# Last three experts of a mixture layer summed by tokens on TensorE, in a one-core hybrid encoder layer

## What is computed

```python
    g_w, g_idx = lax.top_k(group_prob, 1)
    e_w, e_idx = lax.top_k(e_prob, MOE_TOPK)
    weights = g_w * e_w / jnp.sum(e_w)
    hid = silu(h @ w1[e]) * (h @ w3[e])        # 1024 -> 256
    out = sum over the two chosen e of weight * (hid @ w2[e])
    x = x + gt2 * out                          # gt2: a row of 1024, from c
    return rms_norm(x, final_norm_g)
```

## Time and profile before

| | |
|---|---|
| time, median of 3 runs | 794.81 us (790.16 to 795.22) |
| time of the profiled execution | 794.91 us |
| its span, first to last instruction | 792.9 us |
| granted TensorE clock, mean over the span | 0.958 of full |
| TensorE busy | 715.3 us, 90% |
| VectorE busy | 371.7 us, 47% |
| ScalarE busy | 283.9 us, 36% |
| data moved by DMA | 206.94 MB, mean 261 GB/s |

### The profile page before, as it was taken

One profiled execution on the slowest core, in us unless ns is written; L12 is line 12 of the kernel. 1 busy time (PEld: TensorE's weight loads), 2 busy tenths in 40 slices (PEclk: granted clock), 3 DMA queues, 4 the chain that ended last, 5 costly groups with the idle time before them and its releaser, 6 DMA issues.

```text
span 792.9 us, 12682 instructions
## 1 busy us (share of the span) xinstructions
PE 715.3 (90%) x5356; PEld 566.0 (71%) x5356; DVE 371.7 (47%) x648; ACT 283.9 (36%) x406; POOL 43.5 (5%) x39
## 2 busy tenths in 40 slices
PE   9999999999999969889999999989999988888740
PEld 7889999987777757668999998865555554545320
DVE  3476877844564596666677457434201010100006
ACT  2256544565454341243635334332222222222101
POOL 0010000000000714400000000000000000000010
PEclk9999999999999988899999999999999999999985
DMA  9954765755656431222554457968999999999933
GB/s 372 412 199 135 264 238 181 266 212 213 249 218 223 150 117 57 88 74 104 167 207 157 162 195 292 421 273 357 417 422 424 423 421 423 421 424 421 421 88 134
DMA packets 33691, 206.94 MB, mean 261 GB/s; under 512 B 4177, under 2 KB 4561, under 8 KB 10466
## 3 DMA queue, kind: packets, MB, share of 16 engines
q1 hardware_dynamic: 27218, 193.00, 62.7%
q10 hardware_dynamic: 5120, 8.39, 3.0%
q0 software_dynamic: 1296, 4.72, 1.6%
HBM read 194.57 MB, written 11.53 MB: 260 GB/s over the span
## 4 chain that ended last, share of the span: by engine, by line
PE 66%; DMA 18%; DVE 9%; ACT 2%; issue 2%; SPq 2%; DVEq 0%; POOL 0%; ACTq 0%; POOLq 0%
PE ps L1344 65%; DMA r_z<-in_expert_pieces 7%; DMA ring<-in_expert_pieces 4%; DMA r_bt<-in_expert_pieces 4%; SPq L412 2%; DVE ring_rounded L847 2%; ACT ring_rounded L554 2%; DMA ring<-in_pieces 1%; PE ps L1464 1%; DVE r_pv L1033 1%; DVE r_pv L1035 1%; DMA r_lm<-y_rows,r_btm 1%; DMA r_xs<-in_x_t 1%; DVE newton L832 0%; PE ps L1736 0%
## 5 line engine op out<-in xcount | busy, mean ns | idle before, releaser
L847 DVE TENSOR_TENSOR ring_rounded<-ring,ring_rounded 128x2048 fp32r<-128x2048 f32 x60 | 139.6, 2332 | 104.1 <-ACT ring_rounded L554 104.0
L1344 PE MATMUL ps<-hT_rounded,ring_rounded 128*128 128x256 f32 x832 | 156.6, 288 | 0.9 <-DVE ring_rounded L847 0.9
L554 ACT CAST ring_rounded<-ring 128x2048 fp32r<-128x2048 f32 x60 | 114.1, 1903 | 66.8 <-DMA ring<-in_pieces 37.2
L1344 PEld LDWEIGHTS ps<-hT_rounded,ring_rounded 128*128 128x128 f32 x832 | 133.1, 195 | 3.6 <-issue 2.2
L1344 PE MATMUL ps<-x_sb_rounded,ring_rounded 128*128 128x256 f32 x416 | 119.0, 286 | 0.0
L1344 PE MATMUL ps<-ring_rounded,hT_rounded 128*128 128x512 f32 x352 | 111.1, 397 | 0.0
L1287 DVE COPY r_pv<-ps 128x128 f32<-128x128 f32 x32 | 9.3, 292 | 196.4 <-PE ps L1736 196.4
L1344 PEld LDWEIGHTS ps<-x_sb_rounded,ring_rounded 128*128 128x128 f32 x416 | 81.2, 195 | 0.2 <-issue 0.2
L1344 PE MATMUL ps<-ring,r_lm 128*64 128x256 f32 x512 | 67.3, 388 | 13.1 <-DMA ring<-in_expert_pieces 11.0
L1344 PEld LDWEIGHTS ps<-ring_rounded,hT_rounded 128*128 128x128 f32 x352 | 66.1, 190 | 15.3 <-issue 1.8
L1344 PEld LDWEIGHTS ps<-ring,r_lm 128*64 128x64 f32 x512 | 44.1, 140 | 38.0 <-issue 24.2
(11 more groups left out here) (296 smaller groups left out, 1046.1 us busy)
## 6 DMA issues: line engine op xcount, KB each, us to landing
ring<-in_pieces SPq DMA_DIRECT2D x76, 1024.0 KB, 5.0
ring<-in_expert_pieces SPq DMA_DIRECT2D x48, 1024.0 KB, 27.2
r_z<-in_expert_pieces SPq DMA_DIRECT2D x12, 1024.0 KB, 22.5
r_xs<-in_expert_pieces SPq DMA_DIRECT2D x12, 1024.0 KB, 24.2
y_rows<-r_st ACTq DMA_DIRECT2D x64, 128.0 KB, 7.1
g_sb<-in_expert_pieces SPq DMA_DIRECT2D x6, 1024.0 KB, 24.0
r_st<-in_expert_pieces SPq DMA_DIRECT2D x6, 1024.0 KB, 25.4
r_bt<-in_expert_pieces SPq DMA_DIRECT2D x6, 1024.0 KB, 27.8
```

Source lines behind the costliest of these rows:

```text
L554: nc.scalar.copy(high_of(p_), slot_of(p_)).then_inc(hi_ok, 1)
L847: nc.vector.tensor_tensor(low_of(p_), slot_of(p_), high_of(p_).bitcast(F32), ALU.subtract).then_inc(lo_ok, 1)
L1344: return nc.tensor.matmul(o, l, r, start=start, stop=stop)
```

## The change

- Experts 0 to 28 (`EARLY_E` = 29) go the old way, with VectorE in place of ScalarE reading the down product from PSUM; it multiplies by gt2 while it does (`output` is now VectorE's, `gt2_two` holds the row in the layout of `y_row`). ScalarE issues the stores (`store`).
- Experts 29, 30 and 31 are not stored. VectorE makes for them, beside expert 28, weighted one-hot matrices of tokens by slots (`late_pick`: 6 instructions of 128x128 and 4 small ones), TensorE transposes them after the up products of expert 29 (6 transposes into banks 4 and 5), VectorE copies them to `late_rows`, and `scatter(e)` multiplies: 4 products, with 64 rows of weights of 128 columns and 512 columns of the output, accumulated over the three experts in banks 4 to 7. Their input rows in `y_rows` are zero filled beforehand (`ZERO_PARTS`: 6 transfers near 51 us, of which the last is a half, for 4).
- The branch for extra windows stands between expert 28 and expert 29 on TensorE, VectorE and ScalarE. SP waits for the stores up to expert 28, so the gathers are released ahead of the last experts. `y_two` moves to `r_z`.
- The order of TensorE from there is: turn 29, down 29, up 30, scatter 29, turn 30, down 30, up 31, scatter 30, turn 31, down 31, scatter 31. Output 30 waits for `moe_done`.
- VectorE adds the gathered rows of t = 0 to x before output 31, those of t = 1 after it, and then four halves of 128x512 from banks 4 to 7; squares, scalings and the sending of the output go by halves of 512 columns, with one more small addition ahead of the Newton steps.

```diff
+LATE = 3
+EARLY_E = E - LATE
+ZERO_PARTS = ((LATE + JOBS) * W + P - 1) // P
...
-        gt2b = view(r_q, "p d -> p d")
+        gt2_two = r_q[:, 0:CW]
...
-        y_two = view(r_lm, "p (t c d) -> p t c d", t=TT, c=2)
+        y_two = view(r_z, "p (t c d) -> p t c d", t=TT, c=2)
+        late_pick = r_lm[:, 512:512 + LATE * TT * P].rearrange("p (e t h r) -> p e t h r", e=LATE, t=TT, h=2)
+        late_rows = r_lm[:, 1280:1280 + LATE * TT * P].rearrange("p (e t n) -> p e t n", e=LATE, t=TT)
...
-                sp.wait_ge(y_stored[k], 32 * (E // 4))
+                sp.wait_ge(y_stored[k], 32 * len(range(k, EARLY_E, 4)))
             sp.wait_ge(jobs_ok, 1)
-            sp.wait_ge(rows_zeroed, 16 * (JOBS * W // P))
+            sp.wait_ge(rows_zeroed, 16 * ZERO_PARTS)
...
-                sp.wait_ge(fin_done, t + 1)
-                sp.dma_start(out[0, t * P:(t + 1) * P, :], x_sb[:, t]).then_inc(out_done, 16)
-            sp.wait_ge(out_done, 16 * TT)
+                for h in range(2):
+                    sp.wait_ge(fin_done, 2 * t + h + 1)
+                    sp.dma_start(out[0, t * P:(t + 1) * P, h * CW:(h + 1) * CW], x_sb[:, t, h * CW:(h + 1) * CW]).then_inc(
+                        out_done, 16)
+            sp.wait_ge(out_done, 16 * 2 * TT)
...
-            for i in range(JOBS * W // P):
-                pool.dma_start(y_rows[E * W + i * P:E * W + (i + 1) * P, :], zeros).then_inc(rows_zeroed, 16)
+            for i in range(ZERO_PARTS):
+                lo = EARLY_E * W + i * P
+                hi = min(lo + P, (E + JOBS) * W)
+                pool.dma_start(y_rows[lo:hi, :], zeros[0:hi - lo]).then_inc(rows_zeroed, 16)
...
-            def output(e):
-                act.wait_ge(down_full, e + 1)
-                if e >= 2:
-                    act.wait_ge(y_stored[(e - 2) % 4], 32 * ((e - 2) // 4 + 1))
-                nc.scalar.copy(y_row[:, e % 2], ps[2 + e % 2][:]).then_inc(y_out, 1)
+            def store(e):
                 act.wait_ge(y_out, e + 1)
                 for h in range(2):
                     act.dma_start(y_rows[e * W:(e + 1) * W, h * CW:(h + 1) * CW], y_row[h * W:(h + 1) * W, e % 2]).then_inc(
...
-            for e in range(E):
-                if e + 1 < E:
-                    silu_of(e + 1)
+            for e in range(EARLY_E):
+                silu_of(e + 1)
                 if e + 5 < E:
                     rows_of_quarter(e + 5)
-                output(e)
+                store(e)
             act.wait_ge(jobs_ok, 1)
...
-                    act.wait_ge(x_down, j)
-                    nc.scalar.copy(y_row[:, 0], ps[2][:]).then_inc(x_out, 1)
-            for t in range(TT):
-                act.wait_ge(y_sum, t + 1)
-                if t:
-                    act.wait_ge(x3_sq, t)
-                nc.scalar.activation(sq_end, x_sb[:, t], ACT.Square, accum_out=st[:, 4 + t:5 + t]).then_inc(x3_sq, 1)
+            for e in range(EARLY_E + 1, E):
+                silu_of(e)
+            for t in range(TT):
+                for h in range(2):
+                    n_sq = 2 * t + h
+                    act.wait_ge(y_sum, n_sq + 1)
+                    if n_sq:
+                        act.wait_ge(x3_sq, n_sq)
+                    at = 10 + 2 * h + t
+                    nc.scalar.activation(sq_end[:, 0:CW], x_sb[:, t, h * CW:(h + 1) * CW], ACT.Square,
+                                         accum_out=st[:, at:at + 1]).then_inc(x3_sq, 1)
...
+                    half = slice(h * W, (h + 1) * W)
+                    if w == 1:
+                        ins = nc.vector.tensor_copy(gt2_two[half], bank[half, :])
+                    else:
+                        ins = nc.vector.tensor_copy(gt1b[:, h * 512:(h + 1) * 512], bank[:])
+                    ins.then_inc(mix_used(("gtb", w, h)), 1)
...
+            def output(e):
+                dve.wait_ge(down_full, e + 1)
+                if 2 <= e < EARLY_E + 2:
+                    dve.wait_ge(y_stored[(e - 2) % 4], 32 * ((e - 2) // 4 + 1))
+                if e == EARLY_E + 1:
+                    dve.wait_ge(moe_done, 1)
+                if e >= EARLY_E + 2:
+                    dve.wait_ge(late_sum, e - EARLY_E - 1)
+                nc.vector.tensor_tensor(y_row[:, e % 2], ps[2 + e % 2][:], gt2_two, ALU.mult).then_inc(y_out, 1)
+
+            def picks_of_late_experts():
+
+                for t in range(TT):
+                    link(nc.vector.tensor_scalar(ix[:, 6, 0:LATE], ohG[:, 2 * t, EARLY_E:], R[17][:, t, 0:1], None, ALU.mult))
+                    link(nc.vector.scalar_tensor_tensor(late_w[:, t], ohG[:, 2 * t + 1, EARLY_E:], R[18][:, t, 0:1],
+                                                        ix[:, 6, 0:LATE], ALU.mult, ALU.add))
+                    for i in range(LATE):
+                        nc.vector.tensor_scalar(late_pick[:, i, t], count1.unsqueeze(1).to_broadcast([P, 2, W]),
+                                                rank1[:, t, EARLY_E + i:EARLY_E + i + 1], late_w[:, t, i:i + 1],
+                                                ALU.is_equal, ALU.mult).then_inc(late_ok, 1)
+
+            def rows_of_late_experts():
+
+                dve.wait_ge(late_turned, 1)
+                flat = late_rows.rearrange("p e t n -> p (e t n)")
+                nc.vector.tensor_copy(flat[:, 0:512], ps[4][:])
+                nc.vector.tensor_copy(flat[:, 512:], ps[5][:, 0:(LATE * TT - 4) * P]).then_inc(late_back, 1)
+
             hidden(0)
-            for e in range(E):
+            for e in range(EARLY_E):
                 if e % 4 == 2 and e // 4 + 2 < E // 4:
                     pick_quad(e // 4 + 2)
                 hidden_turned(e)
-                if e + 1 < E:
-                    hidden(e + 1)
+                hidden(e + 1)
+                if e == EARLY_E - 2:
+                    picks_of_late_experts()
+                output(e)
...
+            rows_of_late_experts()
             dve.wait_ge(jobs_ok, 1)
             extra = dve.value_load(jobs_i[0:1, JOBS:JOBS + 1], min_val=0, max_val=JOBS)
             with dve.If(extra > 0):
...
-
-            for t in range(TT):
+                    dve.wait_ge(x_down, j)
+                    nc.vector.tensor_tensor(y_row[:, 0], ps[2][:], gt2_two, ALU.mult).then_inc(x_out, 1)
+
+            def add_gathered(t):
                 dve.wait_ge(y_two_ok[t], 32)
-                link(nc.vector.scalar_tensor_tensor(y_two[:, t, 0], y_two[:, t, 1], R[12][:, t, 0:1], y_two[:, t, 0],
-                                                    ALU.mult, ALU.add))
-                link(nc.vector.scalar_tensor_tensor(y_two[:, t, 0], y_two[:, t, 0], R[17][:, t, 0:1], gt2b, ALU.mult,
-                                                    ALU.mult))
-                nc.vector.tensor_tensor(x_sb[:, t], x_sb[:, t], y_two[:, t, 0], ALU.add).then_inc(y_sum, 1)
+                for c_ in range(2):
+                    link(nc.vector.scalar_tensor_tensor(x_sb[:, t], y_two[:, t, c_], R[17 + c_][:, t, 0:1], x_sb[:, t],
+                                                        ALU.mult, ALU.add))
+
+            hidden_turned(EARLY_E)
+            output(EARLY_E)
+            hidden(EARLY_E + 1)
+            hidden_turned(EARLY_E + 1)
+            output(EARLY_E + 1)
+            hidden(E - 1)
+            hidden_turned(E - 1)
+            add_gathered(0)
+            output(E - 1)
+            add_gathered(1)
+            for t in range(TT):
+                for h in range(2):
+                    dve.wait_ge(late_sum, LATE + t)
+                    half = x_sb[:, t, h * CW:(h + 1) * CW]
+                    nc.vector.tensor_tensor(half, half, ps[4 + 2 * t + h][:], ALU.add).then_inc(y_sum, 1)
             dve.wait_ge(s_fng, 16)
-            dve.wait_ge(x3_sq, TT)
+            dve.wait_ge(x3_sq, 2 * TT)
+            link(nc.vector.tensor_tensor(st[:, 4:6], st[:, 10:12], st[:, 12:14], ALU.add))
             rstd(st[:, 4:4 + TT], D)
             for t in range(TT):
-                nc.vector.scalar_tensor_tensor(x_sb[:, t], x_sb[:, t], st[:, 4 + t:5 + t], fng, ALU.mult,
-                                               ALU.mult).then_inc(fin_done, 1)
+                for h in range(2):
+                    half = slice(h * CW, (h + 1) * CW)
+                    nc.vector.scalar_tensor_tensor(x_sb[:, t, half], x_sb[:, t, half], st[:, 4 + t:5 + t], fng[:, half], ALU.mult,
+                                                   ALU.mult).then_inc(fin_done, 1)
...
-            for e in range(E):
-                if e + 1 < E:
-                    up_of(e + 1)
+            def scatter(e):
+
+                pe.wait_ge(y_out, e + 1)
+                if e == EARLY_E:
+                    pe.wait_ge(late_back, 1)
+                for t in range(TT):
+                    for h in range(2):
+                        part = slice(h * W, (h + 1) * W)
+                        ins = mm(ps[4 + 2 * t + h][:], late_rows[part, e - EARLY_E, t], y_row[part, e % 2], e == EARLY_E, e == E - 1)
+                    if t == TT - 1 or e == E - 1:
```

(51 more changed lines are left out.)

## The result

The changed kernel takes 781.54 us (median of 4 runs, 779.96 to 783.95) where the kernel before, run beside it on the same chip, takes 793.59 (4 runs, 790.16 to 795.22): ratio 0.9856, 95% interval 0.981 to 0.9902. Forecast were 786.0 and a range of 782.8 to 790.0.

A forecast was written before the change was run, and what follows sets the result against it. The chain of waits was taken as the bound, with wins only behind 754.5: 13.4 us won after the last down product, 2.8 lost, 794.9 - 10.6 = 784.3, plus 1.7 for a fallen clock = 786.0; range 782.8 to 790.0.

The forecast's parts named there:

- the clock: Between turn 29 and down 29: a 2.0 to 3.1 us gap halves TensorE's clock once, costing 1.7 us; chance 0.37.
- Work ahead of expert 28: Before expert 28: VectorE's output reads, larger zero fill and picks are hidden, costing nothing; 1.2 us if cover were gone.
- Turn 28 to down 29: TensorE after the up products of expert 29: transposes, down 28 ending at 745.5, down 29 starting at 748.2.
- half price of VectorE's branch: Ahead of down 29: VectorE's register load and branch could cost 0 to 1.1 us; half was taken, giving 748.2.
- Down 29 to D: TensorE from down 29 to D, the last down product's end: D at 766.4, 2.8 us later than before.
- The gathers: Released after expert 28's stores at 755.4, first half in at 762.7: hidden with 1.7 us to spare.
- D to the end: From the last down product's end to the kernel's end: 15.9 us instead of 29.3, so 13.4 won.
- the term of the last square: Behind the last down product's end (D): last 128x512 square, 0.63 plus hand-over, follows VectorE's additions, done at D+7.5.
- rival 2: Branch ahead of turn 29 stalls if new instructions must be fetched: 786.6 to 791.6 us; chance 0.10.
- rival 5: From 745.5 to the end of the matmuls the clock stays at 1.2 GHz: 802 us, slower; chance 0.04.
- rival 1: The sum without a fallen clock: 784.3 us; chance 0.27.

The follow-up runs named there:

- before again: The kernel before the change, unchanged, measured once more for its own spread: 790.41 us (8 runs), ratio 0.9981.
- after: The changed kernel as first measured and profiled: 781.54 us, ratio 0.9856 to the kernel before the change; its profiled execution took 780.43.
- no-branch kernel: Changed kernel without the count load, branch and extra-window loop on TensorE, VectorE and ScalarE, and without SP's loop: ratio 0.9849 to the kernel before the change.
- after again: The changed kernel, unchanged, measured and profiled once more: 780.69 us (4 runs), ratio 0.9856 to the kernel before the change.
- two late experts: Changed kernel with experts 30 and 31 summed on TensorE instead of three experts, 29 being stored: ratio 0.9848 to the kernel before the change.
- before: The kernel without the change, run beside the changed one: 793.59 us (4 runs); its first profiled execution took 794.91.
- four late experts: Changed kernel with experts 28 to 31 summed on TensorE and the first gathered half added earlier: ratio 0.9858 to the kernel before the change.
- four, shorter release: Changed kernel with experts 28 to 31 summed on TensorE, SP's count read earlier, a semaphore per gather, gathered passes in VectorE's idle times: 782.8 us, ratio 0.9874.

## Why the prediction was right on where the gain lies and too high in its time

The failed step is the clock: a fall to half clock between turn 29 and down 29 was costed at 1.7 us and measured at nothing. Of the 4.5 us between the 786.0 forecast and 781.54, 1.7 are this term, 1.3 the base of the sum, 0.5 the sum itself, and 1.0 stays open.

The base of the sum was the one profiled execution: 794.91, which I took as typical because the shown median was 794.81. Other sets of the same kernel have medians of 793.59, 791.5 and 791.88. The profiled execution held more low-clock time than before again, and my gain was subtracted from it.

Point by point. Times of after are given on the scale of the forecast, with 3.34 added, by which its transposes at 738.81 stand ahead of the 742.15 of the earlier trace rows.

- **Work ahead of expert 28**: costed at nothing. From the first selection product to turn 28 it grew by 0.85, of which the transposes, forecast in the next step, are 0.7. Right within 0.2.
- **Turn 28 to down 29**: down 28 was to end at 745.5 and did. Down 29 was to start at 748.2 and started at 747.5. The half price of VectorE's branch (0.5) was wrong, it is nothing: the load of the count, 0.54 long at 742.2, lies beside output 28, and the no-branch kernel has the same gap. The second copy took 0.41 as taken.
- **Down 29 to D**: D was to be 766.4 and was 765.4. Down 29 came 0.7 earlier; the rest is overlap of one group of products with the next. The scatters took 1.99, for 1.87 in the sum.
- **The gathers**: forecast hidden with 1.7 to spare, in fact late by 0.55. The store landed after 8.39 us in place of 6.7, above the 6.2 to 7.3 of its neighbours and below the slowest of the earlier trace rows, so the first gathered half was in at 763.9, not 762.7. That the last down product came 1.0 earlier moved up the time at which it was wanted, and took the rest. SP took 1.4 for 1.55, and the gather 7.3 as forecast. The late store was not chance: in after again it took 8.39 too, and VectorE waited 0.90. That a landing of 9.3 would cost at most 1 was not tried.
- **D to the end**: 16.2 for 15.9. Mis-sized is the term of the last square. I had it follow the additions from PSUM (0.69 each, in fact 2.48 for four). But each square of 128x512 is followed by a read of the accumulator, and the four come 0.81 apart:

Timeline of ScalarE after:

```profile
768.79 0.63 ACT L818 ACTIVATE r_xs<-x_sb 128x512 f32<-128x512 f32 x1
769.33 0.19 ACT L818 ACTIVATION_READ_ACCUMULATOR r_xs<-x_sb 128x1 f32 x1
769.61 0.63 ACT L818 ACTIVATE r_xs<-x_sb 128x512 f32<-128x512 f32 x1
```

So ScalarE, not VectorE, sets the pace there, and the Newton steps start at D+8.4, not D+7.5. Of this 0.9 us, 0.45 is the later start of the additions (D+4.4 for D+3.95, since the gathers came late), and 0.7 the squares (VectorE stood idle 1.51 behind its last addition, for 0.8 in the sum), less 0.3 by which the additions were shorter. The output was sent faster, 2.5 for 3.0.

- **The clock**: one stretch at half clock was the likeliest case, at 1.7 us. This is the step that failed. The gap was 1.70, not 2.0 to 3.1, and the clock held; it held for 2.90 too. The earlier trace rows has one fall behind 2.31 and none behind 1.75, which I read as a rule of the gap's length. It is none: 1.97 came with and without a fall, 2.48 came without one where gaps of 2.21 to 2.66 in the other twelve traces had one, and ahead of scatter 31 the changed kernel itself fell behind 1.90 and held behind 2.25 (after and after again). What decides it stays open. The one case in the trace was no ground for a chance of 0.37 against 0.27.
- **The branch** (rival 2). It did not come: TensorE and VectorE show no stall, as the earlier trace rows had none. The Trainium skill ("Runtime: NRT & Kernel Launch", Instruction fetch mechanics) has a taken branch fetch when its target is outside the pages held; no run here shows TensorE or VectorE waiting for such a fetch at this branch, with the loop body in place or left out.
- **Slower by the clock** (rival 5): the clock did fall at the end in the first trace of after, behind the wait of 1.90 for output 31, and in the kernel with two late experts, in an idle time of 4.83. Table by stretches, after:

```profile
764.50:767.00 2.50, 2.50 (x8) 0.69 (x4) 2.43 (x3) 0.00 (x0) 0.00 (x0) 0.50 0.00 0
```

Scatter 31 took 3.48 there in place of 1.99, hidden behind the second gathered half on VectorE, whose sums follow at once at 766.45. My argument against this rival misread the trace of before: ahead of the end of its matmuls it has nine falls, not four, and two of them lasted longer than some 3.5 us (10.2 from 293.3, 6.8 from 320.6).

By size: without the fallen clock the sum was 784.3, a gain of 10.6; the last part gained 11.1. That is rival 1, and its gain was right to 0.5. The measured 781.54 lies 2.8 below 784.3: 1.3 by the base (794.91 for a median of 793.59), 0.5 by the sum, and 1.0 is within what the medians of four runs leave open (the interval of the ratio is 0.0092 wide, 7 us). The difference of the medians is 12.1 in the first comparison and 11.2 in the last (791.88 and 780.69), beside 11.1 in the stretch.

The range failed at its low end. It took in mechanisms that could cost time, up to 790, and on the other side only 1.5 us below the best case, though before's own three runs lay 5 us apart.

## What to carry to other kernels

When results must come back from memory before the end, take the last few pieces of work off that way and finish them on chip: the round trip then runs beside them, and the right number is where its length (here 8.4 for the store, 2.3 to the gather's start, 6.5 for the gather) meets that of the work left. Sum the effect of an edit over the stretch that it changes, and compare that stretch; take the base from the spread of runs, not from the one profiled execution, and let the range reach as far below as that spread. Four small tasks handed from one engine to another run at the pace of the slower one, and its read of an accumulator counts.

## What the runs showed of the hardware that I had not expected

- The order of four products in the lower and upper 64 partitions didn't matter: 1.99 us for a scatter with neighbours in different halves or in the same; 3.70 with all four in one half.
- The granted clock fell at different places, and for 20.5 to 34.1 us in sum ahead of the experts, in thirteen traces of kernels with the same work there but for the zero fill; they start their selection anywhere between 514.1 and 520.6, and start less half of that sum lies between 503.3 and 504.2 in all. An idle time of TensorE of 1.97 us came once with a fall and once without, one of 2.90 without, and one of 2.21 to 2.66 near 699 to 706 with it in twelve traces and without it in one (2.48).
- A store of 128 KB issued while the weight loads fill the DMA engines landed after 8.39 us, the one issued just before it after 7.2; all those issued from 700 to 750 after 6.1 to 8.5.
- Gathers started 8 us (four late experts) and 11 us (four, shorter release) ahead of the up products of expert 31 did not make these wait for weights. The gathers themselves landed later: after 6.6 to 8.4 and 9.3 to 9.7 us, for 5.7 in after, where fewer loads were left.
